# Decoder trunk on one core: low halves of the input weights on GpSimd, and convolution taps earlier on VectorE

## The chip, the cores and the metric

One core of one Trainium2 chip runs the whole program in one launch. The metric is the device time of that launch in microseconds; less is better.

## What is computed

Two decoder layers over 576 tokens: a prompt of 512 and eight samples of 8 tokens each, with shared weights. All data are fp32, and the products are made of two-part operands (below). Of one layer, cut to what matters:

```python
h = x * (1 + sc1) + sh1                       # adaLN
z = h @ w_in                                  # [q | k | v | conv_glu_in], 2560 columns
q, k, v, g = split(z)
o = dilated_attention(rope(q), rope(k), v)    # 8 heads of 64, three dilations
ga, gb = split(g); u = ga * sigmoid(gb)       # 512 channels
cz = silu(layernorm(depthwise_conv31(u)))     # causal, 31 taps
x = layernorm(ALPHA * x + g1 * (concat(rms(o), rms(cz)) @ w_out))
h = x * (1 + sc2) + sh2
x = layernorm(ALPHA * x + g2 * ((silu(h @ w_gate) * (h @ w_up)) @ w_down))
```

## The kernel before

**Weights.** Every 128 output columns of a weight matrix make one unit, 128x1024 fp32. `UL` = 96 units make a layer: 20 of the input projection (`N_IN`: 0 to 7 are the four GLU pairs, 8 to 19 are q, k, v of four head pairs), then `w_out`, gate and up, and down. A unit is fetched by SyncE into one of two raw buffers (`w_raw`, L349), rounded by ScalarE to its high half (`w_hi`, L507), and VectorE subtracts the two for the low half (`w_lo`, L831). There are three buffers of each half. TensorE then makes three products for a unit, high by high, low by high and high by low, 48 matmuls of 128x128 by 128x288 (L1230, for the first two units of a layer L1250). SyncE fetches a unit when the low half two units before is done.

**The loop over input units.** ScalarE and VectorE run `for w in range(1, N_IN)`; iteration w belongs to the end of unit w - 1. ScalarE takes unit w - 1 out of PSUM (the sigmoid of a GLU pair, or q, k into `zraw`, v into `vT`), and then makes the high half of unit w + 2. VectorE, for even w up to 8, makes the GLU product (L1083 to L1086); for w from 9 on it rotates q and k (`rotate`, L999 to L1003). Then it makes the low half of unit w + 2 (`split`), then what the attention wants: for w = 11, 14, 17 the score maxima of a head pair from PSUM (`maxima`, L1014 to L1018, with 2, 2, 2 and 3 taps between its four parts, `TAPS_S`), for w = 12, 15, 18 a reciprocal (L1024) that ScalarE's shares (L588) wait for, and TensorE's turns (L1379) wait for those; for even w up to 8 the convolution of the samples (L891 to L898). Last come `TAPS[w]` taps of the prompt's convolution.

**Taps.** One tap is one instruction over 128x512 (L867 for the first of a tile, L869 for the rest, both inputs in SBUF); four tiles of 31 taps make 124 a layer. The table `TAPS` has one number for each w. What is left after the loop is done in the tail: 8, 8 and 8 taps (`TAPS_TAIL`) and then the rest, between `maxima` of the last head pair, the reciprocals, a low half of `w_out` and the samples' maxima (L1031).

**GpSimd** has adaLN for the samples' columns (L463, L464), two memsets (L482, L483), eight copies of q into `Qz` a layer (`spread_queries`, L475) and sums for the layer norms (L491). Order on every engine is the order in which its block is written; semaphores hold them together: `hi_ready` counts high halves, `lo_ready` low halves, `w_used` units done.

```python
                    if w > QKV0 and (w - 1 - QKV0) % 3 < 2:
                        rotate(l, *divmod(w - 1 - QKV0, 3))
                    if l == 0 and w in (7, 11):
                        ada_bias({7: 2, 11: 3}[w])
                    split(l, w + 2)
```

Of the kernel before, what the change touches and what calls it, by code (L numbers as in the profile page):

```python
# [34 lines left out]
CT = DA // P  # L35
# [18 lines left out]
NR, NW = 2, 3  # L54
N_IN, N_OUT, N_GU = 2 * CT + 3 * CT, KT, 2 * FT
# [5 lines left out]
UL = DN0 + N_DN  # L61
QKV0 = 2 * CT
# [88 lines left out]
def need(eng, sem, n):  # L151

    if n > 0:
        eng.wait_ge(sem, n)


def trunk(nc, xT, cT, ba_d, w_ada, w_mix, w_dn, kc_d, vc_d, st_d, vec_d, rope_d, eye_d, mp_d, msc_d, msn_d,
          y_d, k_d, v_d, cp_d, cs_d):
    with ExitStack() as ctx:
        def sb(name, shape, dt=F32, where=ctx):  # L160
            return where.enter_context(nc.sbuf_tensor("sb_" + name, shape, dt))

        s = {}
# [124 lines left out]
        def by_seq(t):  # L288
            return t.rearrange("p (b t) -> p b t", b=NB)
# [163 lines left out]
        @block.gpsimd  # L453
        def _(pool):
            st = Steps(pool, s["pool_steps"])

            def modulate(l, q):

                for kt in range(KT):
                    hs, xs = by_seq(hf[:, kt % HF, SEQ:T]), by_seq(x[:, kt, SEQ:T])  # L460
                    x_ready(pool, l, q, kt)
                    need(pool, s["h_lo"], (2 * l + q) * KT + kt + 1 - HF)
                    st.link(nc.gpsimd.tensor_tensor(hs, xs, h_mul[:, kt, 1:].unsqueeze(2).to_broadcast([P, NB, NT]), ALU.mult))  # L463
                    nc.gpsimd.tensor_tensor(hs, hs, h_add[:, kt, 1:].unsqueeze(2).to_broadcast([P, NB, NT]), ALU.add)\  # L464
                        .then_inc(s["hs_f"], 1)
# [12 lines left out]
            for l in range(DEPTH):
                modulate(l, 0)

                pool.wait_ge(s["w_used"], l * UL + 1)
                nc.gpsimd.memset(uP[:, :, 0:HIST], 0.0).then_inc(s["hist_zero"], 1)  # L482
                nc.gpsimd.memset(Qz[:], 0.0).then_inc(s["q_zero"], 1)  # L483

                for p in range(CT):
                    spread_queries(l, p)
                for q, z0 in enumerate((Z_OUT, Z_DN)):
                    for m in range(1, KM):
                        pool.wait_ge(z_free[m % 2], z_taken(l, z0, m // 2))
                        st.wait(st.n)  # L490
                        st.of(nc.gpsimd.tensor_tensor(ACC[q][:], (x[:, 0] if m == 1 else ACC[q][:]), x[:, m], ALU.add))  # L491
                    st.restart()
                    pool.sem_inc(s["ln_acc"], 1)
                    if q == 0:
                        modulate(l, 1)
# [324 lines left out]
        def _(dve):  # L820
# [239 lines left out]
            for u in range(2):  # L1060
                split(0, u)

            for l in range(DEPTH):
# [10 lines left out]
                for w in range(1, N_IN):  # L1074
                    if w % 2 == 0 and w <= QKV0:
                        i = w // 2 - 1
                        if w == 2:
                            dve.wait_ge(s["vec_in"], 16 * (l + 1))
                            dve.wait_ge(s["hist"], nth(l, "hist", 15))
                            dve.wait_ge(s["hist_zero"], l + 1)  # L1080
                        computed(l, w - 1)
                        dve.wait_ge(z_free[0], z_taken(l, Z_IN, i))
                        st.of(nc.vector.tensor_tensor(uP[:, i, HIST:HIST + H], Z[1][:, 0], sg[:, 0:H], ALU.mult))  # L1083
                        tap_step[i] = st.of(nc.vector.tensor_tensor(uP[:, i, HIST + H:HIST + SEQ], Z[1][:, 1, 0:HP_], sg[:, H:SEQ],
                                                                    ALU.mult))
                        nc.vector.tensor_tensor(uS[:, i, :, HIST:HIST + NT], by_seq(Z[1][:, 1, HP_:H]), by_seq(sg[:, SEQ:T]),  # L1086
                                                ALU.mult).then_inc(z_free[1], 1)
                    if w > QKV0 and (w - 1 - QKV0) % 3 < 2:
                        rotate(l, *divmod(w - 1 - QKV0, 3))
                    if l == 0 and w in (7, 11):  # L1090
                        ada_bias({7: 2, 11: 3}[w])
                    split(l, w + 2)
                    p, j = divmod(w - QKV0 - 3, 3)
                    if p >= 0:
                        if j == 0:
                            maxima(l, p, TAPS_S)
                        elif j == 1:
                            denominators(l, p)
                        else:
                            if p == 0:  # L1100
                                sample_maxima(l, 0)
                            if p == 2:
                                sample_maxima(l, 1)
                        if (p, j) == (1, 0):
                            sample_denominators(l, 0)
                    if w % 2 == 0 and w <= QKV0:
                        dve.wait_ge(z_free[1], z_taken(l, Z_IN, w // 2 - 1))
                        conv_sample(l, w // 2 - 1)
                    conv_taps(TAPS[w], min(w // 2, CT))

# [49 lines left out]
                for m in range(KT):  # L1160
                    u = OUT0 + m
# [15 lines left out]
                for i in range(FT):  # L1177
                    u = GU0 + 2 * i
# [13 lines left out]
                for m in range(KT):  # L1192
                    for r in range(3):
                        u = DN0 + 3 * m + r
# [481 lines left out]
                norm_last(l, 1)  # L1676


TAPS = [0, 0, 0, 5, 5, 5, 5, 5, 3, 2, 0, 0, 5, 7, 0, 5, 9, 0, 5, 7]
TAPS_S = [2, 2, 2, 3]  # L1680
TAPS_TAIL = [8, 8, 8]

# [94 lines left out]
```

## Time and profile before

| | |
|---|---|
| median of 3 runs | 1647.55 us (1645.03 to 1648.67) |
| the profiled execution, its own time | 1650.15 us |
| its span from first to last instruction | 1648.4 us |
| mean granted clock of TensorE | 0.954 |
| TensorE, matmuls | 1526.2 us busy, 93% of the span |
| VectorE | 790.7 us, 48% |
| ScalarE | 561.6 us, 34% |
| GpSimd | 81.9 us, 5% |
| DMA | 197.16 MB, 120 GB/s on average |

Busy time of an engine is the union of its instructions' times; the chain that ended last is followed back from the last instruction, at each step to what released it or to the instruction before it on its engine. Consecutive instructions of VectorE overlap by some 0.08 us in the records, so the spacing of their starts tells what one costs.

### The profile page before, as it was taken

To read this page: it belongs to the slowest core of one execution; us is meant where nothing else is said; L and a number is where in the kernel's file an instruction comes from. 1 tells how busy PE (TensorE), PEld (TensorE's weight loads), DVE (VectorE), ACT (ScalarE), POOL (GpSimd) and SP (SyncE) were. 2 spreads that over 40 slices of the span, in tenths; PEclk is the share of its full clock that TensorE was granted. 3 is DMA by queue.
4 is the path that set the end of the run, shared out by engine and by line. 5 is a ranking of instruction groups with operands and counts; after the bars stand their busy time and mean duration, and the time that the engine had idled before them with its cause. 6 is when DMAs were issued, how large, how long until landed. Compare 5 with 4: busy or idle time off the path is not lost.

```text
span 1648.4 us, 26440 instructions
## 1 busy us (share of the span) xinstructions
PE 1526.2 (93%) x11456; PEld 1380.1 (84%) x11456; DVE 790.7 (48%) x1246; ACT 561.6 (34%) x884; POOL 81.9 (5%) x104
## 2 busy tenths in 40 slices
PE   5999986889999999999978999868899999999996
PEld 3987754778999999999968977638799999999995
DVE  1789875554222222222327998865643333332233
ACT  3425565234322222211225255652342322221122
POOL 2000000101000000001001000001100000000100
PEclk7999998998999999999987999989889999999998
DMA  9575261422444444452213272512122222222221
GB/s 382 180 143 166 90 269 51 171 80 105 152 153 154 153 148 147 139 184 73 79 54 115 75 131 91 227 68 96 52 64 88 79 80 87 86 78 84 81 71 58
DMA packets 59523, 197.16 MB, mean 120 GB/s; under 512 B 22544, under 2 KB 22928, under 8 KB 48400
## 3 DMA queue, kind: packets, MB, share of 16 engines
q1 hardware_dynamic: 59408, 195.48, 35.7%
q8 instruction: 91, 1.49, 0.4%
q14 instruction: 24, 0.20, 0.0%
HBM read 187.27 MB, written 8.18 MB: 119 GB/s over the span
## 4 chain that ended last, share of the span: by engine, by line
PE 82%; DVE 11%; ACT 3%; issue 1%; DMA 1%; SPq 0%; DVEq 0%; ACTq 0%
PE ps L1230 66%; PE ps L1250 3%; PE ps L1321 3%; DVE sb_y L869 2%; DVE sb_x L980 1%; PE ps L1358 1%; PE ps L1332 1%; DMA sb_big<-w_ada 1%; ACT sb_E L588 1%; PE ps L1379 1%; PE ps L1587 1%; PE ps L1259 1%; DVE sb_x L953 1%; DVE sb_w_lo L831 1%; PE ps L1310 1%
## 5 line engine op out<-in xcount | busy, mean ns | idle before, releaser
L1230 PE MATMUL ps<-sb_h,sb_w_hi 128*128 128x288 f32 x4224 | 766.0, 297 | 3.0 <-DVE sb_x L920 3.0
L1230 PEld LDWEIGHTS ps<-sb_h,sb_w_hi 128*128 128x128 f32 x4224 | 623.1, 188 | 52.0 <-issue 47.4
L1230 PE MATMUL ps<-sb_h,sb_w_lo 128*128 128x288 f32 x2112 | 450.6, 294 | 0.0
L831 DVE TENSOR_TENSOR sb_w_lo<-sb_w_raw,sb_w_hi 128x1024 fp32r<-128x1024 f32 x192 | 235.7, 1229 | 375.5 <-ACT sb_w_hi L507 375.1
L1230 PEld LDWEIGHTS ps<-sb_h,sb_w_lo 128*128 128x128 f32 x2112 | 339.6, 188 | 0.0
L507 ACT ACTIVATE sb_w_hi<-sb_w_raw 128x1024 fp32r<-128x1024 f32 x192 | 202.1, 1053 | 324.1 <-PE ps L1230 290.5
L869 DVE SCALAR_TENSOR_TENSOR sb_y<-sb_uP,sb_vec,sb_y 128x512 f32<-128x512 f32 x240 | 164.8, 743 | 0.5
L1230 PE MATMUL ps<-sb_a_hi,sb_w_hi 128*128 128x288 f32 x704 | 151.9, 296 | 0.0
L1230 PE MATMUL ps<-sb_a_hi,sb_w_lo 128*128 128x288 f32 x704 | 150.1, 294 | 0.0
L1230 PE MATMUL ps<-sb_a_lo,sb_w_hi 128*128 128x288 f32 x704 | 149.6, 293 | 0.0
L795 ACT ACTIVATE sb_a_hi<-sb_af 128x576 fp32r<-128x576 f32 x44 | 30.2, 686 | 267.1 <-DVE sb_af L1185 267.1
L1185 DVE TENSOR_TENSOR sb_af<-ps,sb_gate 128x576 f32<-128x576 f32 x44 | 33.3, 758 | 181.1 <-PE ps L1230 178.8
L1230 PEld LDWEIGHTS ps<-sb_a_hi,sb_w_hi 128*128 128x128 f32 x704 | 112.3, 188 | 7.1 <-issue 6.9
L1230 PEld LDWEIGHTS ps<-sb_a_hi,sb_w_lo 128*128 128x128 f32 x704 | 112.9, 187 | 0.0
L1230 PEld LDWEIGHTS ps<-sb_a_lo,sb_w_hi 128*128 128x128 f32 x704 | 112.8, 187 | 0.0
L790 ACT ACTIVATE sb_gate<-ps 128x576 f32<-128x576 f32 x44 | 28.7, 652 | 162.0 <-PE ps L1230 153.6
L1250 PE MATMUL ps<-sb_h,sb_w_hi 128*128 128x288 f32 x256 | 59.8, 352 | 20.6 <-DVE sb_h L854 20.6
L1250 PEld LDWEIGHTS ps<-sb_h,sb_w_hi 128*128 128x128 f32 x256 | 47.7, 233 | 25.6 <-issue 14.5
L578 ACT ACTIVATE sb_E<-sb_E,sb_small 128x128 f32<-128x128 f32 (+3 forms) x64 | 35.5, 555 | 47.1 <-DVE sb_small L1018 46.4
L1587 PE MATMUL ps<-sb_h,sb_w_hi 128*128 128x288 f32 x128 | 28.0, 343 | 24.3 <-DVE sb_h L1137 16.0
L1187 DVE TENSOR_TENSOR sb_a_lo<-sb_af,sb_a_hi 128x576 fp32r<-128x576 f32 x44 | 33.4, 758 | 33.1 <-ACT sb_a_hi L795 33.1
L1379 PE MATMUL ps<-sb_eye,sb_E 128*128 128x128 f32 x160 | 30.8, 303 | 15.2 <-ACT sb_PT L597 7.0
(195 smaller groups left out, 1309.1 us busy)
## 6 DMA issues: line engine op xcount, KB each, us to landing
sb_w_raw<-w_mix SPq DMA_DIRECT2D x144, 512.0 KB, 3.5
sb_ring<-w_ada SPq DMA_DIRECT2D x40, 1024.0 KB, 5.8
sb_w_raw<-w_dn SPq DMA_DIRECT2D x32, 512.0 KB, 3.5
sb_ring<-vc_d SPq DMA_DIRECT2D x12, 1024.0 KB, 6.9
sb_big<-w_ada SPq DMA_DIRECT2D x8, 1024.0 KB, 12.2
sb_ring<-kc_d SPq DMA_DIRECT2D x8, 1024.0 KB, 7.4
sb_w_raw<-w_dn SPq DMA_DIRECT2D x16, 384.0 KB, 3.2
sb_cache_a<-kc_d SPq DMA_DIRECT2D x4, 1024.0 KB, 8.0
```

Source lines behind the costliest of these rows:

```text
L507: nc.scalar.activation(w_hi[:, g % NW, :], w_raw[:, g % NR, :], ACT.Copy).then_inc(s["hi_ready"], 1)
L578: nc.scalar.activation(blk, blk, ACT.Exp, bias=nm8[p % 2][:, c:c + 1], scale=SCALE, accum_out=den8[p % 2][:, c:c + 1]).then_inc(s["exp_rea ...
L795: nc.scalar.activation(a_hi[:, i], af[:], ACT.Copy).then_inc(s["a_hi"], 1)
L831: nc.vector.tensor_tensor(w_lo[:, g % NW, :], w_raw[:, g % NR, :], w_hi[:, g % NW, :].bitcast(F32), ALU.subtract)\
L869: ins = nc.vector.scalar_tensor_tensor(out=yp, in0=up, scalar=tap, in1=yp, op0=ALU.mult, op1=ALU.add)
L1185: nc.vector.tensor_tensor(halves(af[:]), Z[1], halves(gate[:]), ALU.mult).then_inc(z_free[1], 1)
L1187: nc.vector.tensor_tensor(a_lo[:, i], af[:], a_hi[:, i].bitcast(F32), ALU.subtract).then_inc(s["a_lo"], 1)
L1230: ins = nc.tensor.matmul(z[:, i], a[:, g % NW, w], b[:, k0 + k, i * H:(i + 1) * H], start=first and k == 0 and t == 0, stop=last and k == ...
L1250: ins = nc.tensor.matmul(Z[u][:, i], a[:, j, w], b[:, k, i * H:(i + 1) * H], start=n == 0 and t == 0, stop=n == KT - 1 and t == 2)
L1321: ins = nc.tensor.matmul(ps[j * GW:(j + 1) * GW, ada_banks(sec)[g], :], c_in[:, NG * half + j, :], buf[:, j * 512:(j + 1) * 512], start=ha ...
L1379: ins = nc.tensor.transpose(ps[:, 6 + j % 2, (q - k) * P:(q - k + 1) * P], E[:, e, o:o + P], eye[:])
L1587: ins = nc.tensor.matmul(Z[u][:, i], a[:, j, w], b[:, k, i * H:(i + 1) * H], start=n == 0 and t == 0, stop=n == KT - 1 and t == 2)
```

## The change

In iteration w = 1 to 19 of both layers the low half of unit w + 2 (units 3 to 21) is made by GpSimd and no longer by VectorE, by the same subtraction over the same buffers. GpSimd's copies of q stand among these subtractions, behind that of the iteration, and its two memsets wait for the low half of unit 2. VectorE's remaining low halves wait for all earlier ones, since two engines now raise `lo_ready`. The table `TAPS` has larger numbers, so that more taps are done in the loop; `TAPS_TAIL` is as it was and takes what is left.

```diff
+            def split(l, u):
+
+                g = l * UL + u
+                pool.wait_ge(s["hi_ready"], g + 1)
+                nc.gpsimd.tensor_tensor(w_lo[:, g % NW, :], w_raw[:, g % NR, :], w_hi[:, g % NW, :].bitcast(F32), ALU.subtract)\
+                    .then_inc(s["lo_ready"], 1)
+
...
                 pool.wait_ge(s["w_used"], l * UL + 1)
+                pool.wait_ge(s["lo_ready"], l * UL + 3)
                 nc.gpsimd.memset(uP[:, :, 0:HIST], 0.0).then_inc(s["hist_zero"], 1)
                 nc.gpsimd.memset(Qz[:], 0.0).then_inc(s["q_zero"], 1)
 
-                for p in range(CT):
-                    spread_queries(l, p)
+                for w in range(1, N_IN):
+                    split(l, w + 2)
+                    p, j = divmod(w - QKV0 - 1, 3)
+                    if p >= 0 and j == 1:
+                        pool.wait_ge(s["lo_ready"], l * UL + w + 3)
+                        spread_queries(l, p)
+                        pool.wait_ge(s["qz_ready"], nth(l, "qz_ready", 2 * p + 1))
...
                 dve.wait_ge(s["hi_ready"], g + 1)
+                need(dve, s["lo_ready"], g)
...
-                    split(l, w + 2)
                     p, j = divmod(w - QKV0 - 3, 3)
...
-TAPS = [0, 0, 0, 5, 5, 5, 5, 5, 3, 2, 0, 0, 5, 7, 0, 5, 9, 0, 5, 7]
+TAPS = [0, 0, 0, 6, 7, 6, 7, 6, 5, 5, 4, 2, 7, 8, 2, 8, 11, 2, 8, 9]
```

GpSimd between the memsets and the sums of the layer norm, before:

```order
L482 MEMSET sb_uP 128x4x30 [waits w_used]
L483 MEMSET sb_Qz 128x1024
L475 COPY sb_Qz<-sb_qk 64x4x2x8 [waits q_zero,rope_done]
L475 COPY sb_Qz<-sb_qk 64x4x2x8
L475 COPY sb_Qz<-sb_qk 64x4x2x8 [waits q_zero,rope_done]
```

and changed:

```order
L490 MEMSET sb_uP 128x4x30 [waits lo_ready,w_used]
L491 MEMSET sb_Qz 128x1024
L472 TENSOR_TENSOR sb_w_lo<-sb_w_raw,sb_w_hi 128x1024 [waits hi_ready] x10
L482 COPY sb_Qz<-sb_qk 64x4x2x8 [waits q_zero,rope_done,lo_ready]
L482 COPY sb_Qz<-sb_qk 64x4x2x8
L472 TENSOR_TENSOR sb_w_lo<-sb_w_raw,sb_w_hi 128x1024 [waits hi_ready,qz_ready]
L472 TENSOR_TENSOR sb_w_lo<-sb_w_raw,sb_w_hi 128x1024 [waits hi_ready] x2
```

Ten subtractions stand ahead of the first copies, and three between each pair of copies and the next.

VectorE from the rotation of w = 9 to the first score maximum of w = 11 in layer 0, before:

```order
L1003 TENSOR_TENSOR sb_qk<-sb_zcos,sb_zswap 128x576 [waits dve_steps]
L831 TENSOR_TENSOR sb_w_lo<-sb_w_raw,sb_w_hi 128x1024 [waits hi_ready]
L869 SCALAR_TENSOR_TENSOR sb_y<-sb_uP,sb_vec,sb_y 128x512 [waits dve_steps] x2
L999 STREAM_SHUFFLE sb_zswap<-sb_zraw 128x576 [waits rope_done,z_free1]
L1000 TENSOR_TENSOR sb_zcos<-sb_zraw,sb_rope 128x576
L1002 TENSOR_TENSOR sb_zswap<-sb_zswap,sb_rope 128x576 [waits dve_steps]
L1003 TENSOR_TENSOR sb_qk<-sb_zcos,sb_zswap 128x576 [waits dve_steps]
L831 TENSOR_TENSOR sb_w_lo<-sb_w_raw,sb_w_hi 128x1024 [waits hi_ready]
L991 TENSOR_TENSOR sb_mod<-ps,sb_b_ada 128x72 [waits ada_t]
L831 TENSOR_TENSOR sb_w_lo<-sb_w_raw,sb_w_hi 128x1024 [waits hi_ready]
L1014 ISA sb_E,sb_small<-ps,sb_mp 128x128 [waits s_ps]
```

and changed:

```order
L1017 TENSOR_TENSOR sb_qk<-sb_zcos,sb_zswap 128x576 [waits dve_steps]
L883 SCALAR_TENSOR_TENSOR sb_y<-sb_uP,sb_vec,sb_y 128x512 [waits dve_steps] x5
L1013 STREAM_SHUFFLE sb_zswap<-sb_zraw 128x576 [waits rope_done,z_free1]
L1014 TENSOR_TENSOR sb_zcos<-sb_zraw,sb_rope 128x576
L1016 TENSOR_TENSOR sb_zswap<-sb_zswap,sb_rope 128x576 [waits dve_steps]
L1017 TENSOR_TENSOR sb_qk<-sb_zcos,sb_zswap 128x576 [waits dve_steps]
L883 SCALAR_TENSOR_TENSOR sb_y<-sb_uP,sb_vec,sb_y 128x512 [waits dve_steps] x4
L1005 TENSOR_TENSOR sb_mod<-ps,sb_b_ada 128x72 [waits ada_t]
L1028 ISA sb_E,sb_small<-ps,sb_mp 128x128 [waits s_ps]
```

Three low halves are gone from this piece, and nine taps stand where there were two.

VectorE in the tail, from the last score maximum of head pair 3 on, before:

```order
L1040 RECIPROCAL sb_small<-sb_small 128x1 [waits exps_ready]
L869 SCALAR_TENSOR_TENSOR sb_y<-sb_uP,sb_vec,sb_y 128x512 [waits dve_steps] x8
L1024 RECIPROCAL sb_small<-sb_small 128x8 [waits exp_ready]
L869 SCALAR_TENSOR_TENSOR sb_y<-sb_uP,sb_vec,sb_y 128x512 [waits dve_steps] x8
L831 TENSOR_TENSOR sb_w_lo<-sb_w_raw,sb_w_hi 128x1024 [waits hi_ready]
L1031 ISA sb_Es,sb_small<-ps,sb_msc 128x512 [waits ss_ps,pts_ps]
```

and changed:

```order
L1054 RECIPROCAL sb_small<-sb_small 128x1 [waits exps_ready]
L1038 RECIPROCAL sb_small<-sb_small 128x8 [waits exp_ready]
L845 TENSOR_TENSOR sb_w_lo<-sb_w_raw,sb_w_hi 128x1024 [waits lo_ready,hi_ready]
L1045 ISA sb_Es,sb_small<-ps,sb_msc 128x512 [waits ss_ps,pts_ps]
```

No tap is left in the tail: with the new table all 124 are done by w = 19.

## Rows read from the trace of the kernel before

**Rows 1.** The page: the engines' busy us, and the chain that ended last by line
```profile
PE 1526.2 (93%) x11456; PEld 1380.1 (84%) x11456; DVE 790.7 (48%) x1246; ACT 561.6 (34%) x884; POOL 81.9 (5%) x104
...
PE ps L1230 66%; PE ps L1250 3%; PE ps L1321 3%; DVE sb_y L869 2%; DVE sb_x L980 1%; PE ps L1358 1%; PE ps L1332 1%; DMA sb_big<-w_ada 1%; ACT sb_E L588 1%; PE ps L1379 1%; PE ps L1587 1%; PE ps L1259 1%; DVE sb_x L953 1%; DVE sb_w_lo L831 1%; PE ps L1310 1%
```

**Rows 2.** Stretches: length; PE, PEld, DVE, ACT, POOL busy; clock, DMA share, GB/s
```profile
56.00:119.00 63.00, 63.00 (x476) 55.15 (x476) 55.01 (x77) 19.05 (x24) 1.77 (x2) 1.00 0.58 173
119.00:213.00 94.00, 89.25 (x705) 71.49 (x705) 78.58 (x167) 52.01 (x123) 5.53 (x6) 1.00 0.44 120
...
890.90:948.00 57.10, 57.10 (x432) 56.88 (x431) 55.06 (x79) 19.59 (x23) 1.77 (x2) 1.00 0.35 121
948.00:1042.00 94.00, 88.07 (x690) 70.45 (x690) 80.65 (x168) 52.23 (x123) 5.53 (x6) 0.98 0.47 102
1042.00:1111.00 69.00, 50.42 (x489) 31.36 (x487) 46.88 (x89) 38.30 (x83) 0.00 (x0) 0.88 0.42 168
```

**Rows 3.** Timeline, VectorE, stage A of layer 1: start, duration, count
```profile
904.80 1.23 DVE L831 TENSOR_TENSOR sb_w_lo<-sb_w_raw,sb_w_hi 128x1024 fp32r<-128x1024 f32 x1
905.94 2.29 DVE L891 TENSOR_TENSOR sb_taps<-sb_uS,sb_vec 128x992 f32<-128x992 f32 x2
...
914.87 3.39 DVE L869 SCALAR_TENSOR_TENSOR sb_y<-sb_uP,sb_vec,sb_y 128x512 f32<-128x512 f32 x5
918.18 0.45 DVE L1083 TENSOR_TENSOR sb_uP<-ps,sb_sg 128x288 f32<-128x288 f32 x1
...
918.98 1.21 DVE L831 TENSOR_TENSOR sb_w_lo<-sb_w_raw,sb_w_hi 128x1024 fp32r<-128x1024 f32 x1
```

**Rows 4.** GpSimd's additions by line: busy us, mean ns, idle before
```profile
L491 POOL TENSOR_TENSOR sb_acc_h<-sb_acc_h,sb_x 128x576 f32<-128x576 f32 x6 | 14.7, 2442 | 94.1 <-DVE sb_x L934 94.1
```

**Rows 5.** Timeline of one meeting in layer 0, VectorE and GpSimd
```profile
326.76 2.07 DVE L831 TENSOR_TENSOR sb_w_lo<-sb_w_raw,sb_w_hi 128x1024 fp32r<-128x1024 f32 x1 [0.52 <-ACT sb_w_hi L507]
...
326.32 1.43 POOL L491 TENSOR_TENSOR sb_acc_x<-sb_acc_x,sb_x 128x576 f32<-128x576 f32 x1 [5.19 <-DVE sb_x L920]
```

**Rows 6.** A tap and a copy of 64 columns
```profile
137.89 0.70 DVE L869 SCALAR_TENSOR_TENSOR sb_y<-sb_uP,sb_vec,sb_y 128x512 f32<-128x512 f32 x1
...
138.01 0.68 POOL L475 COPY sb_Qz<-sb_qk 64x64 f32<-64x64 f32 x1
```

**Rows 7.** VectorE on PSUM beside GpSimd
```profile
373.94 0.74 DVE L953 SCALAR_TENSOR_TENSOR sb_x<-ps,sb_x 128x576 f32<-128x576 f32 x1
...
374.16 0.30 POOL L463 TENSOR_TENSOR sb_hf<-sb_x,sb_h_mul 128x64 f32<-128x64 f32 x1 [0.95 <-DVE sb_h L854]
```

**Rows 8.** ScalarE's high halves, stage A of layer 1
```profile
903.71 1.06 ACT L507 ACTIVATE sb_w_hi<-sb_w_raw 128x1024 fp32r<-128x1024 f32 x1 [3.31 <-PE ps L1230]
...
916.40 1.06 ACT L507 ACTIVATE sb_w_hi<-sb_w_raw 128x1024 fp32r<-128x1024 f32 x1 [3.32 <-PE ps L1230]
```

**Rows 9.** VectorE, the last GLU product of layer 1
```profile
932.55 0.45 DVE L1083 TENSOR_TENSOR sb_uP<-ps,sb_sg 128x288 f32<-128x288 f32 x1
```

**Rows 10.** TensorE's first scores of layer 1
```profile
949.57 0.49 PE L1358 MATMUL ps<-sb_qk 64*128 64x128 f32 x4 [1.56 <-issue]
```

**Rows 11.** ScalarE's high halves, stage A of layer 0
```profile
65.70 1.06 ACT L507 ACTIVATE sb_w_hi<-sb_w_raw 128x1024 fp32r<-128x1024 f32 x1 [4.51 <-PE ps L1230]
...
81.67 1.06 ACT L507 ACTIVATE sb_w_hi<-sb_w_raw 128x1024 fp32r<-128x1024 f32 x1 [4.51 <-PE ps L1230]
```

**Rows 12.** Timeline, w = 12 of layer 1: ScalarE and TensorE
```profile
963.29 1.06 ACT L507 ACTIVATE sb_w_hi<-sb_w_raw 128x1024 fp32r<-128x1024 f32 x1 [0.20 <-DMA sb_w_raw<-w_mix]
...
969.46 0.63 PE L1379 MATMUL ps<-sb_eye,sb_E 128*128 128x128 f32 x4 [1.33 <-issue]
```

**Rows 13.** Tail of layer 1: ScalarE, VectorE, TensorE
```profile
1058.92 3.73 ACT L588 ACTIVATE sb_E<-sb_E,sb_small 128x128 f32<-128x128 f32 x8 [1.96 <-DVE sb_small L1024]
...
1072.03 0.69 DVE L1031 CUSTOM_DVE_ANT_0 sb_Es<-ps,sb_msc 128x512 f32<-128x512 f32 x1 [6.75 <-PE ps L1431]
...
1079.78 1.95 PE L1554 MATMUL ps<-sb_sqm,sb_ones 128*128 128x512 f32 x3 [2.74 <-DVE sb_small L1035]
```

## The prediction

> **What bounds the kernel now.** The page comes first: TensorE is busy 93% of the span and holds most of the chain that ended last, but VectorE's tap line (L869, 2%) and its low halves (L831, 1%) stand in that chain too [rows 1]. So shares decide nothing, and the stretches must be read. The table of stretches [rows 2] cuts both layers at the same places: stage A (input units 3 to 10), stage B (units 11 to 19 with the attention beside them), stage C (the tail, where the last head pair and the convolution's norm end). The reader should see that VectorE is idle 63.0 - 55.0 = 8.0 us in stage A of layer 0 but only 2.0 us in the same stage of layer 1, where TensorE has no adaLN matmuls between its units; in stage B it is idle 15.4 and 13.4 us; in stage C 22 us, much of it behind TensorE. Stage A of layer 1 has two engines at their limit, and this is where a change of VectorE's load counts at once.
>
> **What is removed and moved.** Each layer loses 19 low halves on VectorE. Their spacing is 1.14 us (904.80 to 905.94 [rows 3]), so 21.7 us. The sums of the old and new counts (with the 27 taps inside the score maxima of both) give 95 and 124 of 124 taps done before the tail: 29 taps move forward. Five taps take 3.31 us of spacing (914.87 to 918.18 [rows 3]), 0.66 each: 19.2 us. On paper VectorE's time fits, with 2.5 us to spare.
>
> **What is added: GpSimd's subtraction, and the wait it makes.** The nearest operation is its 128x576 addition. The group says 2442 ns [rows 4], one row says 1.43 us [rows 5]. The difference is explained by who ran beside it. At 326.32 it began 0.44 us before VectorE's low half, took 1.43, and VectorE's took 2.07 instead of 1.22; where a low half was already under way the addition took 2.44 [rows 4, 5]. So the two exclude each other: VectorE's 2.07 ends at 328.83, and 1.22 before that is 327.61, so it was held until 1.29 us after GpSimd's start. A tap does the same to a GpSimd copy of 64 columns, which took 0.68 us and ended as the tap did, at 138.69 and 138.59 [rows 6]. An operation that reads PSUM beside one SBUF tile does not: both took their usual 0.74 and 0.30 us while they overlapped [rows 7]. Scaled by 1024/576, a low half on GpSimd takes 2.5 us and holds VectorE's two-input work for 2.3 us. The price of a split therefore lies between 0 (VectorE idle, or on PSUM, a reduction or a shuffle) and 2.3 us, against 1.14 saved.
>
> The Trainium skill (SBUF — State Buffer, Who interferes with whom) states this as a rule against such a change: a VectorE instruction with two SBUF inputs and a GpSimd one that reads SBUF share an exclusive lock, and the later one fully blocks; the trace agrees, by the 2.07 us row. The GPSIMD Engine Reference (3.1) gives 4497 ns for a two-input addition of 2048 columns, 2.25 us for 1024 as an estimate; the trace's 2.5 agrees, and the group mean of 2442 ns, scaled to 4.3 us, would be wrong.
>
> **Stage A, layer 1.** VectorE's period for two units is 14.18 us (904.80 to 918.98 [rows 3]) against TensorE's 12.69 (903.71 to 916.40, two high halves that follow a unit's end [rows 8]). It becomes 14.18 - 2 x 1.14 + 3 x 0.66 = 13.9 us plus one or two holds: 16.2 or 18.5. Two holds fall where VectorE is on time: the even unit's split meets the sample products (two SBUF inputs, 905.94), the odd one's meets taps. When VectorE sets the pace, the odd unit's high half waits for the GLU product and its split falls on the reductions that follow the sample products, so one hold. The GLU product may be late by one unit less itself, 6.35 - 0.80 = 5.5 us, before TensorE waits; it is late by 1.8 now (918.18 against 916.40). So: w = 4, 5 bring 18.5 - 12.7 = 5.8 us of lateness, of which about 0.8 shows; w = 6, 7 bring 16.2 - 12.7 = 3.5, all of which shows. From the GLU product at 932.55 to the first score at 949.57 [rows 9, 10] it takes 17.0 us, with TensorE waiting 1.56; it becomes 17.0 - 2.3 + 5 x 0.66 + 3.5 (one to two holds) = 21.5, and TensorE is there after 0.8 + 12.7 = 13.5: it waits 8.0, 6.4 more than now. Then four taps (2.6 us) and a hold (2.3) stand ahead of the maxima where two low halves (2.3) stood, and the fourth score waits for a maximum: 2 of the 2.6 us show. Sum: 0.8 + 3.5 + 6.4 + 2 = **13 us**.
>
> **Stage A, layer 0.** The pair of units takes 15.97 us (65.70 to 81.67 [rows 11]), so VectorE falls behind by 0.2 to 2.5 us a pair and stays within its slack until the rotation of w = 10. I take 0 for the units and **3 us** for that rotation and the four taps ahead of the maxima.
>
> **Stage B, both layers.** Three times a layer (w = 12, 15, 18) the rotation, a low half, the reciprocal, ScalarE's shares and TensorE's turn form a chain, and TensorE waits 1.33 us in the first [rows 12]. The low half leaves it (-1.14), but the high half ends at 964.35, while the rotation runs (three of its four operations have two SBUF inputs), so GpSimd's hold (+2.3) falls into it: +1.2 each, 3.5 a layer. The rest of the load (11 taps, 7.3; 8 low halves, -9.1; 8 holds of 1.9 or so, 15) is 13 us, what VectorE has idle there; an idle time is never filled without loss, and I add 1.5. **5 us a layer**, 10 in all.
>
> **Stage C.** The 29 taps stood in five places; most were hidden. Seven ahead of the last score maxima become three; those wait for scores anyway, and I put 0.2 us to it. Eight ahead of the reciprocal kept ScalarE idle 1.96 us [rows 13]: that goes. Eight after it, 8 x 0.66 = 5.3 us, are covered by 6.75 us of VectorE's waiting for TensorE: 0. Eight ahead of the last sample maxima, which themselves take some 1.3 us: TensorE has the scores done at 1077.0 and waits 2.74 us for the maxima, to 1079.78 [rows 13]; without taps it waits for the maxima alone, 1.4 us, so 1.3 go. The last five lie under TensorE's fp32 sums from 1079.78: 0. **-3.5 us a layer**, -7 in all. What is late next is the convolution's norm, unchanged.
>
> **The other edits.** The two memsets wait for low half 2, made by VectorE before they start today: 0. GpSimd's copies stand behind a split: they start some 2.5 us later, and the sample scores that need them come three units on: 0. SyncE's fetch of unit w + 4 follows low half w + 2, now some 2 us later after its high half; unit w + 4 is wanted for rounding two units on, 12.7 us later: 0.
>
> **Sum:** 13 + 3 + 10 - 7 = **+19 us** on the profiled execution's 1650.15 us, which lies 2.6 above the median; on the median 1647.55 it makes 1667.
>
> **The rivals.**
> *The holds fall into idle time, and it is faster.* If a split holds VectorE for 0.9 us or less on average, TensorE waits nowhere longer: tail -7, the low half out of the six chains of stage B -6.8, the wait of 1.56 -1.6: -15, 1632. For it: VectorE is idle over half of the span [rows 1], and PSUM reads and reductions aren't held. Against it: 2.0 us idle in stage A of layer 1, and taps are most of what stands there. Chance 0.17. Near its turning point lies no change, 0.05.
> *Every split costs in full.* 38 x (2.3 - 1.14) = 44 us, with no idle time that takes any of it, and -7: +37, 1684. For it: TensorE's stalls come at unit borders, where high halves are made, so splits may keep meeting taps. Against it: VectorE's 39 us of idle time in stages A and B. Chance 0.20.
> *Low halves come too late for TensorE.* A split started at 917.5 ends by 921.2 even behind an operation; its unit starts 12.7 us after 916.4, at 929.1. Margin 8 us. Were the ring of raw weights to run dry instead, each unit would cost up to the 1.3 us that a subtraction is longer, 38 x 1.3 = 49: 1696. Chance 0.03.
> *The forecast,* +8 to +30 us: 0.55.
>
> **The numbers.** 0.2% is 3.3 us, about what a measurement can tell here. Slower 0.78, same 0.05, faster 0.17. The likeliest case alone spans 1655 to 1678. The range reaches half into the fast case and past the full bill: 1640 to 1688.
>
> **What would show it.** Tap rows beside a split of 2 to 3 us instead of 0.75; splits of 2.5 us alone and 3 or more behind a tap; in stage A of layer 1 new waits of TensorE for the GLU product and a wait of some 8 us before the first score; in the tail no tap, and ScalarE's 1.96 gone. Taps at 0.75 us beside splits, or stage A of layer 1 as long as now, would make it wrong.

## The result and the profile after

| | before | after |
|---|---|---|
| median | 1647.26 us (1645.03 to 1648.67, 4 runs) | 1676.1 us (1675.67 to 1676.48, 4 runs) |
| ratio to before | | 1.0176, 95% interval 1.0159 to 1.0194 |
| span of the profiled execution | 1648.4 us | 1674.7 us |
| mean granted clock of TensorE | 0.954 | 0.948 |
| VectorE busy | 790.7 us, 1246 instructions | 808.4 us, 1208 |
| GpSimd busy | 81.9 us | 175.9 us |

The changed kernel is slower by 28.8 us. VectorE has 38 instructions fewer and is busy 17.7 us longer. The page of after, engines, chain and the groups that answer to [rows 1]:

```profile
PE 1529.8 (91%) x11456; PEld 1384.5 (83%) x11456; DVE 808.4 (48%) x1208; ACT 561.0 (33%) x884; POOL 175.9 (11%) x142
...
PE ps L1243 61%; DVE sb_y L883 4%; PE ps L1334 2%; PE ps L1263 2%; PE ps L1371 2%; DVE sb_x L994 1%; PE ps L1444 1%; ACT sb_E L601 1%; DVE sb_taps L905 1%; DMA sb_big<-w_ada 1%; PE ps L1392 1%; PE ps L1600 1%; DMA sb_w_raw<-w_mix 1%; PE ps L1345 1%; DVE sb_y L909 1%
...
L883 DVE SCALAR_TENSOR_TENSOR sb_y<-sb_uP,sb_vec,sb_y 128x512 f32<-128x512 f32 x240 | 183.6, 823 | 0.7
...
L472 POOL TENSOR_TENSOR sb_w_lo<-sb_w_raw,sb_w_hi 128x1024 fp32r<-128x1024 f32 x38 | 98.5, 2593 | 249.8 <-ACT sb_w_hi L520 249.8
```

Taps (L883, L869 before) hold 4% of the chain where they held 2%, their mean is 823 ns, and the sample products (L905) and reductions (L909) are in the chain too. VectorE became the bound of more of the program. Why its busy time grew is read from single meetings. The timeline of after, VectorE and then GpSimd, four places:

```profile
59.25 2.77 DVE L883 SCALAR_TENSOR_TENSOR sb_y<-sb_uP,sb_vec,sb_y 128x512 f32<-128x512 f32 x1
...
203.42 1.87 DVE L1032 TENSOR_SCALAR sb_small<-sb_small 128x2 f32<-128x2 f32 x1
...
910.32 2.47 DVE L912 TENSOR_SCALAR sb_y<-sb_y,sb_vec 128x64 f32<-128x64 f32 x1
...
1001.61 2.94 DVE L1016 TENSOR_TENSOR sb_zswap<-sb_zswap,sb_rope 128x576 f32<-128x576 f32 x1
```
```profile
58.92 2.55 POOL L472 TENSOR_TENSOR sb_w_lo<-sb_w_raw,sb_w_hi 128x1024 fp32r<-128x1024 f32 x1 [5.60 <-ACT sb_w_hi L520]
...
202.90 2.37 POOL L472 TENSOR_TENSOR sb_w_lo<-sb_w_raw,sb_w_hi 128x1024 fp32r<-128x1024 f32 x1 [7.12 <-ACT sb_w_hi L520]
...
910.34 2.39 POOL L472 TENSOR_TENSOR sb_w_lo<-sb_w_raw,sb_w_hi 128x1024 fp32r<-128x1024 f32 x1 [4.41 <-ACT sb_w_hi L520]
...
1000.95 2.98 POOL L472 TENSOR_TENSOR sb_w_lo<-sb_w_raw,sb_w_hi 128x1024 fp32r<-128x1024 f32 x1 [7.51 <-ACT sb_w_hi L520]
```

Every one of these VectorE rows should be 0.17 to 0.76 us. A subtraction that meets nobody takes 2.39 us. The scalar operation at 910.32 ends at 912.79; less its own 0.25 that is 912.54, 2.20 us after the subtraction's start, and at 202.90 the same working gives 2.22. At 1000.95 the subtraction itself first waits through an operation of VectorE (2.98 against 2.39), and the next one of VectorE waits for it. Summed over the operations that overlap the 38 subtractions, what VectorE's take beyond their usual duration is 60.4 us, 1.59 for each subtraction: taps 19.0, the rotation 30.0 (L1014, L1016, L1017), scalar operations 8.2 (L912, L1032), sample products 3.2. Removed were 38 x 1.14 = 43.3. The difference, +17.1, is VectorE's growth of 17.7.

TensorE's waits of after that answer to [rows 10, 12 and 13]:

```profile
129.22 0.58 PE L1371 MATMUL ps<-sb_qk 64*128 64x128 f32 x2 [9.13 <-DVE sb_mod L1005]
...
936.89 0.40 PE L1243 MATMUL ps<-sb_h,sb_w_hi 128*128 128x288 f32 x1 [2.87 <-DVE sb_uS L1100]
...
955.33 0.61 PE L1243 MATMUL ps<-sb_h,sb_w_hi 128*128 128x288 f32 x1 [5.47 <-DVE sb_uS L1100]
...
976.40 0.58 PE L1371 MATMUL ps<-sb_qk 64*128 64x128 f32 x2 [6.41 <-issue]
...
1107.54 0.70 PE L1567 MATMUL ps<-sb_sqm,sb_ones 128*128 128x512 f32 x1 [1.45 <-DVE sb_small L1049]
```

In layer 1 TensorE now waits 2.87 and 5.47 us for GLU products (uS is the last part of one) and 6.41 for the rotated q and k, 14.75 us where there were 1.56 [rows 10]. Layer 0 has a wait of 9.13 us before its first score where there was none over 0.35; it ends with the addition into `sb_mod` (L1005), which stands behind the four taps of w = 10. In the tail the 2.74 of [rows 13] are 1.45. The table of stretches of layer 1, before and then after, cut at the same four events (high half of unit 4, first score of head pair 0, first score of head pair 3, the fp32 sums, the first gated output); the columns are those of [rows 2]:

```profile
890.90:949.60 58.70, 57.14 (x434) 56.94 (x433) 56.62 (x81) 20.78 (x25) 1.77 (x2) 1.00 0.38 123
949.60:1048.40 98.80, 94.43 (x740) 76.63 (x740) 85.42 (x178) 53.89 (x129) 5.53 (x6) 0.98 0.47 109
1048.40:1079.80 31.40, 23.51 (x231) 12.50 (x230) 24.33 (x61) 20.19 (x51) 0.00 (x0) 0.89 0.80 323
1079.80:1136.30 56.50, 41.08 (x327) 32.10 (x328) 30.04 (x31) 24.67 (x40) 0.00 (x0) 0.85 0.01 1
```
```profile
902.30:976.40 74.10, 59.35 (x432) 58.67 (x432) 71.97 (x85) 21.19 (x25) 25.88 (x13) 0.93 0.50 113
976.40:1080.50 104.10, 95.88 (x738) 78.68 (x738) 100.48 (x186) 53.24 (x128) 25.91 (x14) 0.97 0.26 95
1080.50:1107.50 27.00, 22.58 (x230) 12.14 (x229) 8.08 (x34) 20.09 (x50) 0.00 (x0) 0.94 0.89 365
1107.50:1163.50 56.00, 40.54 (x323) 32.69 (x324) 26.91 (x27) 24.72 (x40) 0.00 (x0) 0.82 0.01 2
```

VectorE is busy 72.0 of 74.1 us and 100.5 of 104.1: it is the bound of stages A and B. The same cuts for both layers and several kernels (differences of the starts of those events; E1 to E4 are the experiments below):

| us | before | after | E1 | E2 | E3 | E4 |
|---|---|---|---|---|---|---|
| layer 0, A | 70.0 | 79.4 | 69.6 | 72.4 | 69.6 | 72.2 |
| layer 0, B | 98.4 | 107.7 | 102.2 | 102.9 | 97.3 | 98.8 |
| layer 0, tail to the sums | 31.3 | 27.1 | 33.1 | 27.0 | 27.5 | 31.0 |
| layer 1, A | 58.6 | 74.0 | 66.3 | 66.6 | 59.0 | 66.7 |
| layer 1, B | 98.8 | 104.1 | 104.7 | 105.5 | 98.8 | 98.8 |
| layer 1, tail to the sums | 31.4 | 27.0 | 32.4 | 27.0 | 27.0 | 30.8 |

For the changed kernel these stages add up to +30.8 us, and the spans of the two profiled executions differ by 26.3. The other 4.5 us are won outside the stages: 0.9 ahead of them, 2.2 between layer 0's fp32 sums and unit 4 of layer 1, 1.5 behind layer 1's sums. E1, with the old taps, has 1.4 us of that, E2 and E3, with the new ones, 5.7 and 4.4: most of it goes with the taps that no longer stand in the tail.

### The profile page after: what moved, and what is told of

Its sections match the earlier page's. It is cut to its first block, busy times and chain, and to the rows that moved or that the text cites. A ratio compares the mean times of both kernels' runs of the same rounds, so it can differ in the third digit from the quotient of the medians.

```text
span 1674.7 us, 26601 instructions
## 1 busy us (share of the span) xinstructions
PE 1529.8 (91%) x11456; PEld 1384.5 (83%) x11456; DVE 808.4 (48%) x1208; ACT 561.0 (33%) x884; POOL 175.9 (11%) x142
## 4 chain that ended last, share of the span: by engine, by line
PE 77%; DVE 15%; ACT 3%; DMA 3%; issue 2%; SPq 0%; POOL 0%; DVEq 0%; ACTq 0%; POOLq 0%
PE ps L1243 61%; DVE sb_y L883 4%; PE ps L1334 2%; PE ps L1263 2%; PE ps L1371 2%; DVE sb_x L994 1%; PE ps L1444 1%; ACT sb_E L601 1%; DVE sb_taps L905 1%; DMA sb_big<-w_ada 1%; PE ps L1392 1%; PE ps L1600 1%; DMA sb_w_raw<-w_mix 1%; PE ps L1345 1%; DVE sb_y L909 1%
## 5 line engine op out<-in xcount | busy, mean ns | idle before, releaser
L1243 PEld LDWEIGHTS ps<-sb_h,sb_w_hi 128*128 128x128 f32 x4224 | 627.1, 189 | 60.4 <-issue 47.6
L845 DVE TENSOR_TENSOR sb_w_lo<-sb_w_raw,sb_w_hi 128x1024 fp32r<-128x1024 f32 x154 | 189.2, 1229 | 368.9 <-ACT sb_w_hi L520 368.3
L883 DVE SCALAR_TENSOR_TENSOR sb_y<-sb_uP,sb_vec,sb_y 128x512 f32<-128x512 f32 x240 | 183.6, 823 | 0.7
L472 POOL TENSOR_TENSOR sb_w_lo<-sb_w_raw,sb_w_hi 128x1024 fp32r<-128x1024 f32 x38 | 98.5, 2593 | 249.8 <-ACT sb_w_hi L520 249.8
L504 POOL TENSOR_TENSOR sb_acc_h<-sb_x 128x576 f32<-128x576 f32 x2 | 4.9, 2440 | 665.7 <-DVE sb_x L948 665.7
```

Source lines behind the costliest of these rows:

```text
L472: nc.gpsimd.tensor_tensor(w_lo[:, g % NW, :], w_raw[:, g % NR, :], w_hi[:, g % NW, :].bitcast(F32), ALU.subtract)\
L883: ins = nc.vector.scalar_tensor_tensor(out=yp, in0=up, scalar=tap, in1=yp, op0=ALU.mult, op1=ALU.add)
L1243: ins = nc.tensor.matmul(z[:, i], a[:, g % NW, w], b[:, k0 + k, i * H:(i + 1) * H], start=first and k == 0 and t == 0, stop=last and k == ...
```

## The experiments

The theory on trial (A): a GpSimd operation that reads SBUF holds VectorE for 1.6 us on average, more than the 1.14 saved, and in stage A VectorE has no room for that nor for the moved taps. The rivals are that GpSimd's work costs by something else (any work, a late low half), or that the table of taps alone did it.

### E1 and E2: one half of the change each

E1 is the change with the old table, E2 the kernel before with the new one.

```diff
-TAPS = [0, 0, 0, 6, 7, 6, 7, 6, 5, 5, 4, 2, 7, 8, 2, 8, 11, 2, 8, 9]
+TAPS = [0, 0, 0, 5, 5, 5, 5, 5, 3, 2, 0, 0, 5, 7, 0, 5, 9, 0, 5, 7]
```

> The changed kernel with the old table of taps: GpSimd makes the low halves, no tap moves. Theory A (GpSimd's subtraction and VectorE's two-input work hold each other off, about 2.2 us a meeting): VectorE gets the holds (60 us in both layers with the new taps) against 43 us of low halves saved, with 10.6 us of taps less in stage A of each layer and the tail as before: stage A of layer 1 +4, of layer 0 +1, stage B +4 each, the tail 0: about +13, 1660 us. Rival B (the moved taps alone cost the time, holds are hidden): 1640 to 1645 us.

> The kernel before with the new table of taps alone; VectorE keeps its low halves, GpSimd does none. Theory A: 10.6 us of taps more in stage A meet 2 us of idle time in layer 1 (+9) and 8 in layer 0 (+3), stage B +2 each, the tail -4.4 each: +7 to +9, about 1656 us, and no tap row over 0.8 us. Rival B: all of the change's +29 and so about 1676 us. Rival C (without holds taps are free): 1638 us.

E1: 1667.55 us (1665.81 to 1668.59), ratio 1.0128 (1.0112 to 1.0143). E2: 1657.44 us (1656.17 to 1661.03), ratio 1.0072 (1.0055 to 1.0089). The median before was 1646.56. So the subtractions alone cost 21 us, 7 to 8 more than expected, and the taps alone 11. Summed the same way as above, E1's VectorE was held 63.8 us against 43.3 saved, +20.5. By the table E1's excess over its forecast lies in stage A of layer 1 (7.7 us, forecast 4) and in the tails (2.8 in both, forecast 0). E2 has TensorE waiting at two of the three places of layer 1, with no subtraction on GpSimd:

```profile
936.33 0.42 PE L1230 MATMUL ps<-sb_h,sb_w_hi 128*128 128x288 f32 x1 [2.88 <-DVE sb_uS L1086]
...
955.72 0.58 PE L1358 MATMUL ps<-sb_qk 64*128 64x128 f32 x2 [4.89 <-issue]
```

Both halves load the same full engine. Together they cost 29 and not 32, but stage by stage they don't add: stage A of layer 0 is 9.4 us longer in the changed kernel where E1 and E2 together give 2.0, stage B of layer 1 is 5.3 longer where they give 12.6. In E1 the tail keeps its taps, in E2 and after it gets 4.2 to 4.4 us shorter a layer.

### E3: the same GpSimd time, without its reads

Each subtraction is replaced by three fills. The low halves of input units 3 to 21 are left out of the computation (zeros).

```diff
-                nc.gpsimd.tensor_tensor(w_lo[:, g % NW, :], w_raw[:, g % NR, :], w_hi[:, g % NW, :].bitcast(F32), ALU.subtract)\
-                    .then_inc(s["lo_ready"], 1)
+                for n in (UNIT, UNIT):
+                    st.link(nc.gpsimd.memset(w_lo[:, g % NW, 0:n].bitcast(F32), 0.0))
+                nc.gpsimd.memset(w_lo[:, g % NW, 0:512].bitcast(F32), 0.0).then_inc(s["lo_ready"], 1)
```

> The changed kernel, but in place of each of its 38 subtractions GpSimd fills the buffer with zeros three times (128x1024, 128x1024, 128x512), some 2.5 us in all, without reading SBUF; the low halves of input units 3 to 21 are left out thereby. All waits and the time at which TensorE gets its buffer stay about as they are. Theory A (the hold comes with GpSimd's reading): VectorE is 43 us lighter and is held nowhere, the tail's 9 us are won: 1632 to 1640 us. Rival D (low halves come too late, by waits or by the raw ring): 1676 us, as changed. Rival E (any GpSimd work on SBUF holds VectorE): 1665 to 1676 us.

1635.49 us (1634.18 to 1636.44), ratio 0.9933 (0.9919 to 0.9948). The groups of E3, fills and taps:

```profile
L473 POOL MEMSET sb_w_lo<- 128x1024 f32 x76 | 72.8, 958 | 218.6 <-ACT sb_w_hi L521 216.4
L474 POOL MEMSET sb_w_lo<- 128x512 f32 x38 | 20.0, 526 | 2.2
...
L884 DVE SCALAR_TENSOR_TENSOR sb_y<-sb_uP,sb_vec,sb_y 128x512 f32<-128x512 f32 x240 | 164.6, 743 | 0.7
```

The low half comes 2.4 us after its high half, as in the changed kernel, GpSimd is as busy there, the taps stand where the change puts them, and the mean tap is 743 ns. 41 us separate this kernel from the changed one, so low halves that come late for TensorE or for the fetches are excluded as its cause, and so is any large cost of GpSimd's work that isn't its reading (the fills lengthen three scalar operations, by 1.4 us in all; see the last section). It is also the time the change would have if nobody was held, 1635; the fast rival had forecast 1632.

### E4 and E5: subtractions that nobody needs

E4 adds to the kernel before ten GpSimd subtractions a layer of a constant tile from itself, each begun when a high half is ready; only the scaling of the first turned scores waits for the last. E5 has three fills in their place.

```diff
+                for w in range(1, 11):
+                    pool.wait_ge(s["hi_ready"], l * UL + w + 3)
...
+                    nc.gpsimd.tensor_tensor(PT[:, 0, 0:UNIT], r, r, ALU.subtract).then_inc(s["side"], 1)
```

> The kernel before, untouched on VectorE, ScalarE and TensorE but for one wait; GpSimd subtracts a 128x1024 piece of a constant from itself into a buffer that is unused then, ten times a layer, when the high half of units 3 to 12 is ready; nothing waits for it in stage A. Theory A: seven of ten meet two-input work and hold it 2.2 us, 15 us a layer; layer 1 has 2 us idle for it and shows 13, layer 0 has 8 and shows 6: about +19, 1666 us. Rival B: 1647 us, no difference.

> As the run with GpSimd's subtractions on the side (1657.9 us), but each of the twenty is three fills with zeros, which read nothing. Theory A (a GpSimd instruction must read SBUF to hold VectorE): 1647 us, as before, no tap over 0.8 us. Rival E (any GpSimd instruction holds): 1655 us or more.

E4: 1657.91 us (1656.86 to 1659.18), ratio 1.0070 (1.0055 to 1.0085), median before 1646.94. E5: 1648.06 us (1647.45 to 1650.65), ratio 1.001 (1.0001 to 1.0019). E4's meeting at 114 us, and the group of its subtractions:

```profile
114.06 2.11 POOL L491 TENSOR_TENSOR sb_PT<-sb_rope 128x1024 f32<-128x1024 f32 x1 [5.65 <-ACT sb_w_hi L515]
```
```profile
114.33 3.04 DVE L878 SCALAR_TENSOR_TENSOR sb_y<-sb_uP,sb_vec,sb_y 128x512 f32<-128x512 f32 x2
```

Two taps take 3.04 us where two take 1.40. E4's subtraction reads one tile twice; alone it takes 1.90 us and not 2.39, and it holds VectorE until some 1.7 us after its start. VectorE was held 18.8 us by 20 of them, and the kernel lost 11.0: less than the 19 expected, because the operation was shorter, and layer 0 took only 2.2 + 0.4 us of it (the table). Reading costs 10 us and filling 1: the theory's mechanism is seen by itself, with nothing that depends on GpSimd's result.

### E8: the same subtraction in two halves

```diff
-                nc.gpsimd.tensor_tensor(w_lo[:, g % NW, :], w_raw[:, g % NR, :], w_hi[:, g % NW, :].bitcast(F32), ALU.subtract)\
+                st.link(nc.gpsimd.tensor_tensor(w_lo[:, g % NW, 0:512], w_raw[:, g % NR, 0:512], w_hi[:, g % NW, 0:512].bitcast(F32), ALU.subtract))
+                nc.gpsimd.tensor_tensor(w_lo[:, g % NW, 512:], w_raw[:, g % NR, 512:], w_hi[:, g % NW, 512:].bitcast(F32), ALU.subtract)\
```

> The changed kernel with each of GpSimd's 38 subtractions in two of 512 columns, each with a completion wait. Theory A: the hold is by instruction, so each is about 1.1 us, VectorE gets one operation in between, and the sum of the holds stays near 60 us: 1670 to 1680 us. If a long hold at a bad place was what cost the time: 1660 us or less.

1671.38 us (1669.62 to 1676.2), ratio 1.0154 (1.0138 to 1.017): the median is 4.7 us better than the changed kernel's, though one of its four runs took 1676.2, and VectorE is busy 800.6 us, 7.8 less. A half is 1.29 us alone. Most of them met somebody, and one was itself locked out:

```profile
L472 POOL TENSOR_TENSOR sb_w_lo<-sb_w_raw,sb_w_hi 128x512 fp32r<-128x512 f32 x38 | 64.4, 1696 | 218.3 <-ACT sb_w_hi L521 218.3
L473 POOL TENSOR_TENSOR sb_w_lo<-sb_w_raw,sb_w_hi 128x512 fp32r<-128x512 f32 x38 | 62.2, 1636 | 3.0
```
```profile
75.05 6.38 POOL L472 TENSOR_TENSOR sb_w_lo<-sb_w_raw,sb_w_hi 128x512 fp32r<-128x512 f32 x1 [4.53 <-ACT sb_w_hi L521]
```

A smaller piece moves some of the holding from VectorE to GpSimd, where it costs nothing while the low half isn't late. At 60.4 - 7.8 = 52.6 us the holds still exceed the 43.3 saved.

### E9 and E10: what a wait of TensorE costs beside its length

In the changed kernel stage B of layer 0 is 9.2 us longer, and TensorE's waits in it only 4.1 (8.8 where they were 4.75). The granted clock there was lower. So in the kernel before, the first score of layer 0 was made to wait for GpSimd fills that begin behind a high half near 114 us: fifteen in E9, nine in E10. VectorE's and ScalarE's work is as before.

```diff
+                    if l == 0 and p == 0:
+                        pool.wait_ge(s["hi_ready"], 13)
...
+                        for _ in range(15):
+                            st.link(nc.gpsimd.memset(PT[:, 0, 0:UNIT], 0.0))
+                        pool.sem_inc(s["side"], 1)
...
+                        pe.wait_ge(s["side"], 1)
```

> Fifteen fills of 1024 columns on GpSimd (0.96 us each, they read nothing and hold nobody) start behind the high half that ends at 115.1 us in layer 0, and TensorE's first score waits for the last of them, about 9 us longer than in the kernel before; VectorE's and ScalarE's work is untouched. (A) A wait of this length also costs TensorE its clock: the granted clock of the 35 us behind the wait falls to about 0.85, and the kernel is slower by 9 plus 3 to 5 us, less some 1 us that later waits for VectorE give back: 1657 to 1661. (B) The 0.85 seen in the changed kernel had another cause, and the wait costs its own length or less: clock 1.00 behind it, 1654 to 1656.

> The same with nine fills: TensorE's first score of layer 0 comes about 3 us later. (A) If the clock falls with the length of the wait, little is lost beside the wait: clock 0.95 to 1.00 behind it, 1649 to 1652. (A2) If any wait of some us costs the same stretch at the lower clock, it is 3 plus 3 to 5 us: 1653 to 1655. (B) Only the wait: 1648 to 1650.

E9: 1659.1 us (1657.45 to 1660.45), ratio 1.0072 (1.0058 to 1.0085). E10: 1652.3 us (1650.38 to 1653.66), ratio 1.0028 (1.0018 to 1.0038); median before 1647.79. The stretches behind the first score, of before (one), of after and of E9 (three each) and of E10 (two):

```profile
120.60:151.00 30.40, 28.70 (x219) 24.20 (x217) 27.09 (x59) 17.49 (x41) 1.84 (x2) 1.00 0.70 166
```
```profile
129.20:134.00 4.80, 4.78 (x22) 3.97 (x23) 2.14 (x8) 0.88 (x4) 0.00 (x0) 0.59 0.92 381
134.00:150.00 16.00, 13.97 (x97) 12.08 (x96) 15.19 (x32) 7.30 (x20) 2.57 (x1) 1.00 0.11 35
150.00:165.00 15.00, 14.12 (x104) 10.98 (x104) 14.60 (x24) 8.09 (x19) 4.33 (x3) 0.77 0.44 176
```
```profile
129.00:134.00 5.00, 4.98 (x20) 3.93 (x20) 1.99 (x7) 0.88 (x4) 0.00 (x0) 0.50 0.89 369
134.00:150.00 16.00, 14.66 (x101) 12.73 (x100) 14.72 (x33) 8.36 (x22) 1.84 (x2) 0.98 0.10 25
150.00:165.00 15.00, 15.00 (x125) 11.80 (x124) 13.01 (x27) 9.06 (x20) 0.00 (x0) 1.00 0.50 191
```
```profile
123.40:126.80 3.40, 3.40 (x15) 3.18 (x16) 1.99 (x7) 0.88 (x4) 0.00 (x0) 0.50 1.05 118
126.80:165.00 38.20, 36.87 (x268) 28.88 (x266) 33.20 (x74) 20.18 (x50) 1.84 (x2) 1.00 0.45 166
```

Behind a wait of 9.74 us E9's TensorE runs some 5.5 us at 0.50, that is 1.2 GHz; behind one of 3.69 us E10's runs 3.4 us so. In the changed kernel it is 3.9 us behind the wait of 9.13 and, from 150.2 us on, 6.8 more, behind its next wait, 2.91 us at 150.88 where the kernel before has 1.37. What this costs is read from the way from pair 0's first score to pair 1's, less TensorE's waits in it:

| us | before | E10 | E9 | after |
|---|---|---|---|---|
| first score of pair 0 to that of pair 1 | 30.38 | 30.82 | 31.72 | 35.46 |
| of it TensorE waits | 1.70 | 1.33 | 1.34 | 2.91 |
| of it at half clock | 0 | 3.4 | 5.5 | 10.7 |
| way less waits, over that of before | | 0.8 | 1.7 | 3.9 |

So of the changed kernel's 5.1 us on this way 1.2 are waits, and 3.9 go with the lower clock. The expectations held in part. E9's median is what its (A) expected, but its clock over the 35 us behind the wait is 0.92 and not 0.85, and the way of the trace is only 1.3 us longer where (A) had 3 to 5. The medians' 11.3 exceed the 10.5 by which the trace's way to the fp32 sums is longer (9.3 to the first score, 1.2 behind it); that much is within the spread of the runs. E10's median lies 0.3 above the range of its (A) and under that of (A2); its trace is (A)'s, clock 0.95 over 35 us. What makes the second fall of the changed kernel as long as 6.8 us is open: at the same turn E2 has 3.4 us at half clock, behind a wait of 2.53 us.

### E6 and E7: what could be had without GpSimd

Does the tail's gain come from the order of its taps? E6 is the kernel before with `TAPS_TAIL` = [0, 21, 0]: none ahead of the reciprocal and none ahead of the sample maxima. E7 also moves three taps of w = 8 and 9 behind the first scores, to w = 15 and 18.

```diff
-TAPS = [0, 0, 0, 5, 5, 5, 5, 5, 3, 2, 0, 0, 5, 7, 0, 5, 9, 0, 5, 7]
+TAPS = [0, 0, 0, 5, 5, 5, 5, 5, 2, 0, 0, 0, 5, 7, 0, 6, 9, 0, 7, 7]
...
-TAPS_TAIL = [8, 8, 8]
+TAPS_TAIL = [0, 21, 0]
```

> The kernel before with TAPS_TAIL = [0, 21, 0] for [8, 8, 8]: no tap moves out of the tail, but the eight ahead of the reciprocal and the eight ahead of the last sample maxima stand behind the reciprocal, where VectorE waits for TensorE. If the tail's gain of the change came from those two places, it comes here too, without GpSimd: 2.0 + 1.3 us a layer, 1640 us. If it needs the tail free of taps: 1647 us.

> As the run before it, and three taps of w = 8 and 9 go to w = 15 and 18, so that VectorE reaches the rotation of w = 10 two us sooner: the wait of 1.56 us before the first score of layer 1 goes, stage B has room for the taps: 1638 to 1639 us. If stage B has no room: 1640 us or more.

E6: 1639.85 us (1637.9 to 1642.78), ratio 0.9958 (0.9946 to 0.9971). E7: 1638.55 us (1637.05 to 1638.8), ratio 0.9948 (0.9934 to 0.9961); both are faster than either kernel; between E6 and E7 the measurement can't tell, though in E7's trace the wait of 1.56 us before the first score of layer 1 is gone. E6's tail of layer 1:

```profile
1072.67 3.70 PE L1554 MATMUL ps<-sb_sqm,sb_ones 128*128 128x512 f32 x8 [1.46 <-DVE sb_small L1035]
```
```profile
1051.30 3.73 ACT L588 ACTIVATE sb_E<-sb_E,sb_small 128x128 f32<-128x128 f32 x8
```

ScalarE's wait of 1.96 us is gone and TensorE's 2.74 is 1.46, as in the changed kernel, with 29 of 29 taps still in the tail. But the whole of the tail's gain isn't there: E6's tails are 28.2 and 29.9 us, 3.1 and 1.5 shorter than before, where the changed kernel's are 4.2 and 4.4 shorter. The 21 taps behind the reciprocal now stand ahead of the sample maxima, and TensorE has a new wait behind ScalarE's sample exponentials, 1.15 us in layer 0 and in layer 1 this one:

```profile
1066.74 0.86 PE L1447 MATMUL ps<-sb_eye,sb_Es 128*128 128x128 f32 x4 [2.24 <-ACT sb_Es L618]
```

So about half of the part of the change that paid needed neither GpSimd nor earlier taps; the rest came with the taps that left the tail.

## Why the prediction came out as it did

The median forecast was 1667 us (+19) and the result is 1676.1 (+28.8): slower, by the mechanism forecast, and within 1655 to 1678, the likeliest case's own range. Point by point, in differences of the stages between the profiled executions:

- **The subtraction's time and hold: right.** 2.5 and 2.3 us were forecast; 2.39 and 2.20 to 2.22 were measured. Taps of 2.8 us beside splits stand in the timeline. The copy of [rows 6] was held as it was read: one that meets no tap takes 0.23 us (E3 at 143.44).
- **Stage A of layer 1: the mechanism right, the size low.** Of the 13 us forecast 10.7 lie ahead of the first score, where +15.5 was measured; the 2 us put to the fourth score's wait for a maximum didn't come, TensorE has no such wait over 0.3 us. The new waits are 14.75 - 1.56 = 13.2 us. Their places are those named: two GLU products (0.8 and 3.5 forecast, 2.87 and 5.47 measured) and the first score (8.0 forecast, 6.41). The rest of the stage is a clock of 0.93 where it was 1.00.
- **Stage A of layer 0: the step that failed, 3 forecast, +9.4 measured.** The step put "0 for the units" because VectorE's slack would take the lateness. The wait before the first score is 9.13 us, where it was none. VectorE's timeline of after, from the second GLU product to the fourth:

```profile
65.09 0.45 DVE L1097 TENSOR_TENSOR sb_uP<-ps,sb_sg 128x288 f32<-128x288 f32 x1
...
66.00 4.50 DVE L905 TENSOR_TENSOR sb_taps<-sb_uS,sb_vec 128x992 f32<-128x992 f32 x2
...
74.01 11.65 DVE L883 SCALAR_TENSOR_TENSOR sb_y<-sb_uP,sb_vec,sb_y 128x512 f32<-128x512 f32 x11
85.59 0.45 DVE L1097 TENSOR_TENSOR sb_uP<-ps,sb_sg 128x288 f32<-128x288 f32 x1
...
104.12 0.45 DVE L1097 TENSOR_TENSOR sb_uP<-ps,sb_sg 128x288 f32<-128x288 f32 x1
```

The two pairs take 20.5 and 18.5 us, where the step had 16.2 to 18.5 against TensorE's 16.0: the first had three holds (one in the sample products, two in the taps), 6.5 us, and not one or two. So VectorE is some 7 us late at the last GLU product, two more holds follow in the rotations, and the four taps stand ahead of what the first score waits for. The sum was made pair by pair and its lateness not carried to the end of the stage, as it was for layer 1. E1, with the holds and the old taps, keeps 69.6 us and E2, with the taps alone, has 72.4: the holds alone stay within the slack, the taps alone exceed it by 2.4, both together by 9.4.
- **Stage B: +5 a layer forecast, +9.2 and +5.3 measured.** Layer 1 is right: at its three turns TensorE waits 1.4 to 1.6 us longer each, for which 1.2 was forecast. In layer 0 the waits are 4.1 us more; of the other 5.1, 3.9 go with the lower clock on the way to pair 1, a term that the sum didn't have. E9 and E10 show such a loss without the change, 1.7 and 0.8 us; that it grows to 3.9 is read from the clock's rows only.
- **The tail: right.** -3.5 a layer forecast, -4.2 and -4.4 measured. In layer 1 TensorE's waits of over 0.25 us fell from 7.6 to 4.3 us; the rest goes with a clock of 0.94 where it was 0.89. E6 shows about half of the gain by itself. Behind the sums, where the prediction put 0, the new table seems to have won some 3 us more in both layers together, by a comparison of single profiles.
- **"One or two holds" a pair: too few kinds of operation.** The prediction counted operations with two SBUF inputs. Scalar operations with one were held as well, 8.2 of the 60.4 us. The average hold of 1.59 us is inside the 0 to 2.3 of the bounds; the rival "every split costs in full" had 2.3, and the fast rival's limit was 0.9.
- **Not every saved microsecond was worth one.** The low half of unit 3 stood where VectorE waits anyway, for a high half and then for the transfer into `uS` ahead of the first GLU product: its waits there were 14.6 us in both layers together and are 17.4. The subtractions of unit 3 held nobody, and the low half taken from VectorE gained nothing.
- **The rivals.** E3 gives the fast one, 1635, under the condition that nobody is held, and rules out late low halves.

## What to carry to other kernels

Before work goes from VectorE to GpSimd, multiply the time that GpSimd spends reading (here 2.2 us) by the share of it that falls on VectorE's work in SBUF (here 1.59 / 2.2, 0.72), and compare with the time saved (1.14): from about one half on it is a loss. Work that doesn't read SBUF cost little there: twenty groups of fills 1.1 us of 1647 (E5). And when a stage is slower by a little on both of two causes, add both to the same slack, to the stage's end: one alone may be hidden or nearly so (layer 0: E1 -0.4 us, E2 +2.4) and the two are not (+9.4).

## What the runs showed that was not expected

- **Scalar operations with one SBUF input are held.** L912 takes 0.25 us alone and 2.47 at 910.32, L1032 0.17 and 1.87. The Trainium skill (SBUF — State Buffer, Who interferes with whom) names `tensor_scalar` among the operations that can run in a mode that uses both ports, and says that in such a mode VectorE contends with GpSimd, without the limit to GpSimd's reads that it gives for two SBUF inputs. This case's trace agrees: in E3 scalar operations are the ones that a mere fill lengthens (L913 takes 0.83 us at 58.45, and 0.25 alone), while the taps beside the fills are not held. The reductions (L909) kept their 2.27 us for two beside subtractions.
- **GpSimd may get in between VectorE's operations, or not.** Split times run from 2.34 to 3.45 us in the changed kernel, and one half in E8 took 6.38 beside a run of taps. What decides it no run here shows.
- **A subtraction of one tile from itself is cheaper** than one of two tiles of the same size: 1.90 us against 2.39 (E4).
- **TensorE's clock can fall to 1.2 GHz even behind a short wait.** It ran so for 5.5 us behind 9.74 us (E9), for 3.4 behind 3.69 (E10), and in E2 for 3.4 behind the 2.53 us that end at 141.52, but not behind the 2.64 us that end at 121.94.
